# GpSimd makes the low parts of the second and third weight unit at the head of two attentions and two projections

## The reference, cut to what matters

```python
# first block, for each of two layers
x = x + 0.5 * swiglu(rms_norm(x, norm_ffn1[l]), ...)
x = x + hybrid_mixer(rms_norm(x, norm_mix[l]), w_in[l], ..., w_ck1[l], ..., w_cv1[l], ..., w_out[l], cos, sin)
x = x + 0.5 * swiglu(rms_norm(x, norm_ffn2[l]), ...)
# hybrid_mixer: proj = h @ w_in; compressed keys and values are gelu(flat @ w_ck1) @ w_ck2 and
# gelu(flat @ w_cv1) @ w_cv2, where flat is made from columns of proj

# second block, for each of two layers
h = rmsnorm(x, norm1_g[l])
p = h @ w_in[l]          # feeds an RWKV-7 branch, a retention branch, a gating unit and three gates
...
x = x + conv_ffn(rmsnorm(x, norm2_g[l]), ...)
```

## Time and profile before

| what | us |
|---|---|
| median of three runs | 2054.05 |
| the profiled execution | 2055.12 |
| its span, from first to last instruction | 2053.0 |
| TensorE (PE) busy | 2006.0 (98%) |
| weight loads of TensorE (PEld) busy | 1859.5 (91%) |
| VectorE (DVE) busy | 1350.8 (66%) |
| ScalarE (ACT) busy | 1008.9 (49%) |
| GpSimd (POOL) busy | 13.0 (1%) |

### The profile page before, as it was taken

One profiled execution on the slowest core, in us unless ns is written; L12 is line 12 of the kernel. 1 busy time (PEld: TensorE's weight loads), 2 busy tenths in 40 slices (PEclk: granted clock), 3 DMA queues, 4 the chain that ended last, 5 costly groups with the idle time before them and its releaser, 6 DMA issues. The chain is left out here.

```text
span 2053.0 us, 41611 instructions
## 1 busy us (share of the span) xinstructions
PE 2006.0 (98%) x17544; PEld 1859.5 (91%) x17544; DVE 1350.8 (66%) x2078; ACT 1008.9 (49%) x1458; POOL 13.0 (1%) x12
## 2 busy tenths in 40 slices
PE   8999999999999999999999999999999989999998
PEld 8999987999999998799989889989998978998997
DVE  6554676654755477675558676578767856578775
ACT  6333466543634255663346444466446534457443
POOL 0000000000000000000000000000000010000000
PEclk9999999999999999999999999999999999999999
DMA  8543731654464372354454334366534423357551
GB/s 308 199 188 114 254 129 69 266 201 157 166 243 184 134 234 91 126 226 185 157 184 154 124 109 136 122 241 243 195 134 167 156 75 119 122 187 262 196 184 52
DMA packets 79876, 348.77 MB, mean 170 GB/s; under 512 B 21232, under 2 KB 30576, under 8 KB 45808
## 3 DMA queue, kind: packets, MB, share of 16 engines
q1 hardware_dynamic: 79728, 346.61, 46.4%
HBM read 345.53 MB, written 1.05 MB: 169 GB/s over the span
## 5 line engine op out<-in xcount | busy, mean ns | idle before, releaser
L88 PE MATMUL bank<-ffn_hT_split,n_split_gate_up 128*128 128x256 f32 x1280 | 354.3, 277 | 0.0
L89 PE MATMUL bank<-ffn_hT_split,n_split_gate_up 128*128 128x256 f32 x1280 | 353.8, 276 | 0.0
L90 PE MATMUL bank<-ffn_hT_split,n_split_gate_up 128*128 128x256 f32 x1280 | 353.7, 276 | 0.0
L89 PEld LDWEIGHTS bank<-ffn_hT_split,n_split_gate_up 128*128 128x128 f32 x1280 | 240.5, 188 | 1.5
L88 PEld LDWEIGHTS bank<-ffn_hT_split,n_split_gate_up 128*128 128x128 f32 x1280 | 240.4, 188 | 1.5
L90 PEld LDWEIGHTS bank<-ffn_hT_split,n_split_gate_up 128*128 128x128 f32 x1280 | 240.3, 188 | 0.0
L409 ACT ACTIVATE work<-bank 128x256 f32<-128x256 f32 x88 | 32.8, 382 | 280.8 <-PE bank L90 276.2
L1929 DVE TENSOR_TENSOR mix_parts<-mix_arrived,mix_parts 128x1024 fp32r<-128x1024 f32 x88 | 107.6, 1224 | 92.2 <-ACT mix_parts L1924 92.0
L551 DVE TENSOR_TENSOR work<-bank,work 128x256 f32<-128x256 f32 x88 | 37.2, 423 | 178.6 <-ACT work L409 178.6
L532 DVE TENSOR_TENSOR ffn_split_down<-ffn_arrived_down,ffn_split_down 128x2048 fp32r<-128x2048 f32 x44 | 100.8, 2292 | 79.6 <-ACT ffn_split_down L390 79.6
L486 DVE TENSOR_TENSOR n_split_gate_up<-arrived_gate_up,n_split_gate_up 128x2048 fp32r<-128x2048 f32 x60 | 135.9, 2287 | 11.6 <-ACT n_split_gate_up L380 11.6
(11 more groups left out here) (418 smaller groups left out, 5954.5 us busy)
## 6 DMA issues: line engine op xcount, KB each, us to landing
arrived_gate_up<-in_ffn SPq DMA_DIRECT2D x64, 1024.0 KB, 8.6
ffn_arrived_down<-in_ffn SPq DMA_DIRECT2D x44, 1024.0 KB, 4.8
mix_arrived<-in_mix_w SPq DMA_DIRECT2D x88, 512.0 KB, 3.6
rrived_gate_up<-in_conv_ffn SPq DMA_DIRECT2D x32, 1024.0 KB, 6.8
_arrived_gate_up<-in_ffn SPq DMA_DIRECT2D x24, 1024.0 KB, 6.7
mixer_arrived<-in_w_in SPq DMA_DIRECT2D x22, 1024.0 KB, 7.3
onv_ffn_arrived_down<-in_conv_ffn SPq DMA_DIRECT2D x22, 1024.0 KB, 4.8
irst_project_arrived<-in_w_in SPq DMA_DIRECT2D x17, 1024.0 KB, 4.9
```

The lines of the kernel that those rows point to most:

```text
L88: pe.matmul(out, lhs[0], rhs[0], start=start, stop=False)
L89: pe.matmul(out, lhs[0], rhs[1], start=False, stop=False)
L90: return pe.matmul(out, lhs[1], rhs[0], start=False, stop=stop)
```

## The change

GpSimd waits for the low part of unit 0 and then makes those of units 1 and 2. VectorE no longer makes them; before it makes the low part of unit 3 it waits until three low parts are there, so that `unit_split` keeps counting in order. The same is done in both kinds of phase, and GpSimd's stream gets the projections' part behind what it had.

```diff
@@ nsa_phase
     def gpsimd(pool):
         pool.wait_ge(ph.prev.s["act_ready"], ph.prev.n0["act_ready"] + 2 * N_CHUNK)
         pool.memset(c.hid, 0.0).then_inc(s["pad_ready"], 1)
+        pool.wait_ge(s["unit_split"], n0["unit_split"] + 1)
+        for n in range(1, RING):
+            ring.low(pool, n, width(n))
@@ nsa_phase, vector
         def low_after(i):
             unit = jobs[i][0]
             if i == last_job[unit]:
+                if unit == 0:
+                    dve.wait_ge(s["unit_split"], n0["unit_split"] + RING)
                 ring.low(dve, unit + RING, width(unit + RING))
@@
         turned_low_vector(dve, c, FIRST_BANKS, ph, c.hT_parts[:, 0], c.hT_parts[:, 1])
-        for n in range(1, RING):
-            ring.low(dve, n, width(n))
@@ rw_project_phase
+    def gpsimd(pool):
+        pool.wait_ge(s["unit_split"], 1)
+        for n in range(1, RING):
+            ring.low(pool, n)
@@ rw_project_phase, vector
         def low_after(i):
             n = jobs[i][0] + RING
             if i == last_job[jobs[i][0]] and n < N_UNITS:
+                if n == RING:
+                    dve.wait_ge(s["unit_split"], RING)
                 ring.low(dve, n)
@@
         turned_low_vector(dve, c, FIRST_BANKS, ph, c.hT_parts[:, 0], c.hT_parts[:, 1])
-        for n in range(1, RING):
-            ring.low(dve, n)
@@ the two blocks
             nsa1.gpsimd(pool)
             nsa2.gpsimd(pool)
+            project.gpsimd(pool)
...
                 scan_mix.gpsimd(pool)
+                if not last:
+                    project.gpsimd(pool)
```

More of the change, by code:

```diff
@@ L2262, in vector_norm @@
         norm_vector(dve, c, ph, t)
-    ph.sync, ph.scalar, ph.vector, ph.tensor = sync, scalar, vector, tensor
+    ph.sync, ph.gpsimd, ph.scalar, ph.vector, ph.tensor = sync, gpsimd, scalar, vector, tensor
     ph.vector_split, ph.vector_norm = vector_split, vector_norm
```

## The result

The changed kernel takes 2057.78 us (median of 20 runs) against 2054.39 us for the kernel before (20 runs beside them). The ratio is 1.0023 with a 95% interval of 1.0016 to 1.0030: 4.7 us slower, between 3.3 and 6.2. The plain difference of the two medians is 3.4 us and that of the two means 4.0, both inside this interval. The forecast was 3.4 us slower, 2057.4. Three single executions among all those of this study took 3308, 3991 and 6519 us, where every other took 2047 to 2067; they are left out of the ratios.

The account below looks back on a forecast made before the run. TensorE, busy 98% of the span, was taken as the bound. Terms 1.62 + 2.19 + 0 - 0.40 = 3.4 us slower made the forecast 2057.4 us from a median of 2054.05; range 2053.0 to 2060.5.

Parts of the forecast that it names:

- GpSimd's duration: One low-part subtraction on GpSimd: 4.45 us, the middle between two and three memset passes, against VectorE's 2.29.
- The three terms that grow with it: Both landings of `w_cmp1` in the attentions and job 2 of the second projection grow one for one with GpSimd's duration.
- Rival B: GpSimd's subtraction is slower than 4.45 us; loss passes 4.1 us at 4.68, reaches 6.4 us at 5.34; 22%.
- rival C: GpSimd's subtraction is faster: at 3.56 us the kernel loses 1.1 us, at 1.78 it gains 0.97; 10%.
- Unit 1 for job 2: Job 2's start: attentions lose 0.42 and 0.63 us, first projection nothing, second projection gains 0.40.
- The train: Attention loads from unit 4 on, with `w_cmp1`, run 2.16 us late; `hidden_columns` loses 1.62 and 2.19 us.
- A step that I put at nothing: Units 4, 5 and 6 land 2.16 us late, but their readers are late by then: nothing added.
- The added wait on VectorE: VectorE waits for GpSimd's second low part before unit 3's; job 6, SyncE and the projections' `mix` lose nothing.
- unit 2: Unit 2 for job 4: ready at 214.34 in the first attention, job 4 started at 215.30; no loss.
- the first projection: Unit 1 ready for job 2 at 1074.57, before its start at 1075.19: no gain or loss.
- The 0.72 us of the first attention: Slack between the landing of `w_cmp1`'s second half at 228.81 and `hidden_columns` at 229.53, before the change.
- Rival D: A stall of 2 us or more in the second attention also lowers TensorE's clock: 3 us on top, 2060.4; 3%.

Follow-up runs that it names:

- late_unit4: Kernel before, all low parts on VectorE; SyncE waits in the attentions for three low parts, not two, before issuing unit 4. Ratio 1.0023 (1.0012 to 1.0034).
- half_early: Changed kernel with only the first half of `w_cmp1` issued ahead of unit 4. Ratio 1.0000; repeated for its profile, 0.9999, both to the kernel before.
- attention_only: Changed kernel with the projections' part undone, so only the attentions are changed. Ratio to the kernel before 1.0021 (1.0011 to 1.0032).
- beside: Changed kernel with two more VectorE instructions in each attention during GpSimd's low part of unit 1. One execution for its trace; the two-input one took 5.11 us.
- early_cmp: Changed kernel with both halves of `w_cmp1` issued ahead of unit 4. Ratio to the kernel before 1.0007 (0.9994 to 1.0021).
- projection_only: Changed kernel with the attentions' part undone, so only the projections are changed. Ratio to the kernel before 0.9994 (0.9982 to 1.0005).
- mix_first: Kernel before, without GpSimd; in the projections VectorE does `mix(0)` between the low parts of units 1 and 2. Ratio 1.0001 (0.9992 to 1.0010).
- second_only: Changed kernel with GpSimd making unit 2's low part alone and VectorE unit 1's, at all four heads. Ratio to the kernel before 0.9997 (0.9985 to 1.0008).

## Why the prediction was right

**GpSimd's duration** was taken as 4.45 us from the memset rows and measured 4.62. The three terms that grow with it make 3 x 0.17 = 0.5 us: 3.4 becomes 3.9. The Trainium skill's 4497 ns for a two-input add ("GPSIMD Engine Reference", "Elementwise — side-by-side cycle accounting") is 3% below this row. Rival B decided from 4.68 on and rival C needed 3.56 or less; the duration lies between them. That it came so near is in part luck: no row stood behind the middle between two and three passes, and no run here shows that GpSimd's time goes by passes.

**Unit 1 for job 2** was right at each head within 0.04 us (table above), but by two errors that nearly cancel. The duration was 0.16 us too short, and the time from the release to the matmul, taken as 0.18 us from VectorE's `mix`, was 0.05 us behind GpSimd (its first low part ends at 205.07 + 4.61 = 209.68, the matmul starts at 209.73) and 0.06 in the second projection. There the stall changed hands as said: 0.80 us behind VectorE became 0.54 behind GpSimd, where 0.4 was forecast.

**The train** was right in size and place. Counted from the first low part, unit 4 is issued 2.3 us later in both attentions (forecast 2.16), and the second half of `w_cmp1` lands 2.1 and 2.4 us later. There is no bubble at unit 5: in windows of 2 us from 212 to 230 us the DMA share is 0.96 to 1.24, at 301 to 413 GB/s. `late_unit4` shows that it makes the loss by itself, `half_early` that the loss goes with it.

**Where the trace looks other than forecast.** I expected idles of 1.2 and 1.6 us before `hidden_columns`, and they are 0.88 and 0.94. The landing sets when `hidden_columns` starts, so what TensorE loses on the way only comes off that idle. In the second attention it lost some 0.7 us: jobs of 24 matmuls follow each other every 2.72 us before and every 2.82 after (below), over seven jobs. In the profiles of `attention_only` and `beside`, whose second attentions kept 2.72, this idle is 1.62 us, as forecast. The loss of 2.43 us is as large as forecast nonetheless.

**A step that I put at nothing and that isn't.** Of units 4, 5 and 6 I said that their readers are late by then. ScalarE reads unit 5 with the copy of job 6 queued behind, and in the first attention of three of the kernels (`late_unit4`, `beside`, `attention_only`) job 8 waited 0.8 to 1.0 us for that. It added nothing to the sum only because the second half of `w_cmp1`, on the same train, ends later still. In `early_cmp`, where that cover was taken away, such a wait appeared at once, there for unit 4.

**The added wait on VectorE, unit 2, the first projection** cost nothing in the attentions and in this profile. The slack of the first projection's job 2, forecast 0.6 us, is thin: in the profile of `half_early_again` TensorE waits 0.8 us there for GpSimd. It goes with how soon TensorE's clock is back at 2.4 GHz behind the long norm: its granted clock read 0.50 for about 3.5 us there, and for about 7 us in the profiles before and after, where job 2 did not wait.

**What stays open.** The landmarks give 3.6 us and the runs 4.7 (3.3 to 6.2); `attention_only` and `late_unit4` lie at 4.3 and 4.7 too. The intervals hold both numbers. Part of the gap is a slack that I read off one execution. The 0.72 us of the first attention belong to a profile in which its jobs came every 2.82 us. In `projection_only` and `mix_first`, with the same code there, they came every 2.72 us; `hidden_columns` began 23.68 and 23.46 us after the first low part, not 24.09, and had waited for the DMA. Against the mean of those two the changed kernel loses 2.0 us in the first attention and not 1.51, and the sum becomes 4.1.

Rival D was given 3% and is not in the sum. The clock did not fall in the attentions of the changed kernel's profile, but it did in that of `late_unit4`, so some executions may lose more by it; how often, one profile for each kernel can't tell. Whether the rest of the gap is real was not settled, nor whether the second projection's share can be measured at all.

## What to carry to other kernels

When a step is moved to a slower engine, look not only at who reads its result but at what else its semaphore releases: here the slower low part delayed a queue of loads, and a weight that had nothing to do with it set the time. Slack of a DMA train is read from the landing of its last member against its reader, and in more than one execution: here the same code had 0.72 us of slack in one and none in two others. The train was bound by bandwidth and kept the time by which it started late. Where loads are moved ahead of such a train, look at what then stands behind them: with one half of `w_cmp1` ahead no load was late, with both halves unit 4 was.

## What the hardware showed beyond expectation

**Two spacings at one granted clock.** ScalarE's copies show how jobs of 24 matmuls follow each other. First attention before, second attention before, second attention after:

```profile
212.68 0.39 ACT L1027 ACTIVATE raw<-bank 128x256 f32<-128x256 f32 x1 [0.64 <-PE bank L90]
215.50 0.39 ACT L1027 ACTIVATE raw<-bank 128x256 f32<-128x256 f32 x1 [2.44 <-PE bank L90]
...
734.16 0.38 ACT L1027 ACTIVATE raw<-bank 128x256 f32<-128x256 f32 x1 [0.53 <-PE bank L90]
736.88 0.38 ACT L1027 ACTIVATE raw<-bank 128x256 f32<-128x256 f32 x1 [2.34 <-PE bank L90]
```

```profile
739.37 0.39 ACT L1030 ACTIVATE raw<-bank 128x256 f32<-128x256 f32 x1 [2.44 <-PE bank L90]
...
742.19 0.39 ACT L1030 ACTIVATE raw<-bank 128x256 f32<-128x256 f32 x1 [0.64 <-PE bank L90]
```

A job takes 2.72 us or 2.82 us, all at a granted clock of 1.00, and keeps its spacing until TensorE does something else. I had tied the longer one to a stall ahead of it, in two of the expectations. That is not so: the second projection had 2.82 in `second_only` with no stall at job 2, and 2.72 in the changed kernel with a stall of 0.54. Which one a run of jobs gets differs between executions and heads, and what decides it is open. Over six or seven jobs it is 0.6 to 0.7 us, as much as the waits that this study is about.

**VectorE and GpSimd share a read path.** A `tensor_tensor` of 128x512 with both inputs in SBUF took 5.11 us beside GpSimd's subtraction and a `tensor_scalar` with one input 0.43 us. The Trainium skill says so in "SBUF — State Buffer", section "SBUF: two separate sides": a VectorE instruction with two SBUF inputs contends with a GpSimd instruction that reads SBUF, and the later one blocks for the whole of the other. The trace agrees: VectorE's instruction, which started second at 205.98, ended 0.54 us after GpSimd's at 210.55.
